# One hybrid decoder step: the first norm by sums of squares per token, and the dt products between the first chunk's two units

## The chip, the cores and the metric

The kernel runs on one core of a Trainium2 chip. The metric is the device time of one execution in microseconds (us), lower is better.

## The reference

The kernel computes two layers over 320 tokens (256 of a prompt, 64 of samples) of width 1024, in float32. Cut to what matters here:

```python
def rmsnorm(x, g):
    y = xf * lax.rsqrt(jnp.mean(xf * xf, axis=-1, keepdims=True) + EPS)
    return (y * g.astype(jnp.float32)).astype(x.dtype)

def parallel_mixer(hn, ...):
    proj = jnp.einsum('bld,de->ble', hn, w_in)          # 1024 x 3592
    q, f, i, og, z, xbc, dt = jnp.split(proj, SPLIT_IDX, axis=-1)   # dt: the last 8 columns
    ...
def trunk(...):
    for l in range(DEPTH):                              # 2 layers
        mix, ... = parallel_mixer(rmsnorm(h, norm_mix[l]), ...)
        h = h + mix
        hn = rmsnorm(h, norm_ffn[l])
        h = h + (swiglu(hn, ...) if l % 2 == 0 else moe_swiglu(hn, ...))
    return rmsnorm(h, norm_final), ...
```

## The kernel before

Activations lie transposed: `xT` has the 1024 features as 8 groups of 128 partitions and the 320 tokens as columns. Each engine has its own written-out list of instructions (`block.sync`, `gpsimd`, `scalar`, `vector`, and TensorE), and the lists meet only at counting semaphores `S(name)`. So the order of the lines of an engine is the order of its work, and a wait holds everything behind it on that engine.

**Weights** come in units of 1 MB through a ring of six buffers. SyncE's queue loads unit `u` (L435). ScalarE copies it to `spH`, rounded to the high part (`split_hi`, L591), VectorE subtracts to get the low part `spL` (`split_lo`, L944), and the next load into that buffer waits for `split_done`. `spH` and `spL` have two buffers each: `split_hi(u)` waits until TensorE has used unit `u-2`. A product is then three matmuls: high weights with `hnH` (L1505) and with `hnL` (L1506), low weights with `hnH` (L1584). A chunk of `w_in` is 512 output columns, two units of 512 input rows each; a layer has seven chunks (function `dense` on TensorE, 32 + 32 matmuls of high weights and 32 of low ones in a chunk). Of chunks 0 and 1 VectorE makes a convolution of four taps (L1046, L1049), which ScalarE then passes through Silu (L694, L695). Chunk 2 is the first without one.

**The start.** SyncE loads the three tiles of tokens `xin` (128, 128 and 64 tokens, L424), then units 0 and 1, then the table `stage` and the rest of `tab` (L428, L429), then units 2 and on. TensorE waits for all three tiles (`x_in` 48), transposes them in six groups of four into two PSUM banks in turn (L1549), and ScalarE copies each group to `xT` (L626). TensorE then turns two small arrays of vectors (`vin`, L1555; norm weights among them), of which layer 1's come by GpSimd's queue and layer 0's by ScalarE's (L392).

**A norm before** (`norm_t` on ScalarE and VectorE, `norm_mm` on TensorE): ScalarE squares four groups of `xT` and VectorE four. Then both split two units of weights (`before_rstd`). TensorE sums the squares over the partitions with eight float32 matmuls of a matrix of ones (L1521). ScalarE makes `rstd` from it (L606, L607). VectorE multiplies `xT` by the norm weight and `rstd` (eight instructions, L955). ScalarE copies the two halves to `hnH` (L610), VectorE subtracts to get `hnL` (L962).

**The dt products** (`narrow`, L1499 to L1501): 24 matmuls of 8 weight columns (`wnH`, `wnL`) with `hnH` and `hnL`. They stand ahead of chunk 0 on TensorE, and they wait for `setup_dve` 2, that is `wnL` (L982). Ahead of them stand eight small transposes of the convolution's state `cst` (L1563). At the end of chunk 0 their result is turned (L1538).

ScalarE rounds the table `stage` to `tabR` (L645) right after the first norm and its small set-up copies, ahead of the loading of the Silu table. TensorE needs `tabR` after the seven chunks (L1620).

## Time and profile before

| what | before |
|---|---|
| median of 3 executions | 1950.88 us (1950.7 to 1952.35) |
| the profiled execution, its own time | 1948.23 us |
| its span in the profile | 1946.5 us, 1.73 us less than its time |
| share of TensorE, VectorE, ScalarE in the chain that ended last | 89%, 7%, 2% |
| TensorE busy with matmuls | 1838.4 us, 94% of the span |
| VectorE busy | 1338.6 us, 69% |
| ScalarE busy | 1046.1 us, 54% |
| GpSimd busy | 85.1 us, 4% |
| mean granted clock of TensorE | 0.953 of full |

The first layer's input projection ends near 140 us and the second layer starts near 572 us; from about 890 us the experts run. A busy TensorE is not TensorE at its peak: at the lower clock the same matmul takes about twice as long. Times in the rows are from the start of the span.

### The profile page before, as it was taken

The page shows a single profiled execution, that of the slowest core. Times are in us where ns is not written, and L with a number is a line of the kernel's source. Part 1 is how long each engine was busy: PE and PEld are TensorE (multiplying, and loading weights), DVE is VectorE, ACT ScalarE, POOL GpSimd, SP SyncE. Part 2 cuts the span into 40 slices and gives each one's busy share as a digit, 9 for nine tenths or more (in the row PEclk, how much of TensorE's full clock was granted, in tenths as well). Part 3 has the DMA queues.
Part 4 walks back from the last instruction along what each step waited for, and adds up shares of the span by engine and source line. Part 5 has one row for each costly group of instructions (what it writes and reads, how often), then busy time and mean ns, then how long its engine had stood idle before and what let it go on. Part 6 is the DMA issues. An engine that isn't in the chain of part 4 may idle for free.

```text
span 1946.5 us, 25826 instructions
## 1 busy us (share of the span) xinstructions
PE 1838.4 (94%) x9949; PEld 1601.0 (82%) x9949; DVE 1338.6 (69%) x1160; ACT 1046.1 (54%) x924; POOL 85.1 (4%) x93
## 2 busy tenths in 40 slices
PE   6998988999889998987999999999999999999996
PEld 5997867999889988876888888888888888888885
DVE  3635554444355345536988889889888898888987
ACT  3443323333333442234677767776677767776775
POOL 2002120000000011211000000000000000000000
PEclk9998878999999978787999999999999999999998
DMA  7432134443462412135999999999999999999994
GB/s 241 140 123 55 35 95 132 146 147 115 120 190 87 152 41 54 45 103 201 338 364 326 355 340 344 367 331 353 364 330 353 328 354 368 327 351 334 353 357 146
DMA packets 267900, 452.62 MB, mean 233 GB/s; under 512 B 41258, under 2 KB 102946, under 8 KB 267832
## 3 DMA queue, kind: packets, MB, share of 16 engines
q1 hardware_dynamic: 266192, 448.83, 66.5%
q0 software_dynamic: 1376, 2.67, 0.7%
q8 instruction: 48, 0.79, 0.2%
q10 hardware_dynamic: 264, 0.17, 0.1%
q14 instruction: 20, 0.16, 0.0%
HBM read 440.66 MB, written 10.97 MB: 232 GB/s over the span
## 4 chain that ended last, share of the span: by engine, by line
PE 89%; DVE 7%; ACT 2%; issue 1%; DMA 1%; POOL 0%; SPq 0%; DVEq 0%; ACTq 0%
PE ps L1510 16%; PE ps L1511 16%; PE ps L2038 11%; PE ps L1505 8%; PE ps L1506 7%; PE ps L2053 5%; PE ps L1584 3%; PE ps L1969 3%; PE ps L1693 3%; PE ps L1678 2%; DVE cvt L1049 1%; PE ps L1984 1%; PE ps L2081 1%; DVE spL L944 1%; PE ps L1848 1%
## 5 line engine op out<-in xcount | busy, mean ns | idle before, releaser
L1401 DVE TENSOR_TENSOR spL<-ring,spH 128x2048 fp32r<-128x2048 f32 x339 | 771.5, 2292 | 113.0 <-ACT spH L873 112.9
L873 ACT ACTIVATE spH<-ring 128x2048 fp32r<-128x2048 f32 x339 | 648.6, 1916 | 124.9 <-PE ps L2053 64.8
L1510 PE MATMUL ps<-spH,XH 128*128 128x512 f32 x896 | 356.8, 398 | 1.5 <-DVE XL L1407 1.5
L1511 PE MATMUL ps<-spH,XL 128*128 128x512 f32 x896 | 352.0, 393 | 0.0
L944 DVE TENSOR_TENSOR spL<-ring,spH 128x2048 fp32r<-128x2048 f32 (+1 forms) x74 | 158.4, 2147 | 238.0 <-ACT spH L591 237.9
L1505 PE MATMUL ps<-hnH,spH 128*128 128x320 f32 x928 | 276.8, 313 | 13.7 <-DVE hnL L962 7.1
L1506 PE MATMUL ps<-hnL,spH 128*128 128x320 f32 x928 | 275.3, 311 | 0.0
L591 ACT ACTIVATE spH<-ring 128x2048 fp32r<-128x2048 f32 (+1 forms) x74 | 132.6, 1798 | 246.5 <-PE ps L1584 107.8
L2038 PE MATMUL ps<-spL,XH 128*128 128x512 f32 x896 | 241.8, 392 | 0.0
L1510 PEld LDWEIGHTS ps<-spH,XH 128*128 128x128 f32 x896 | 168.9, 188 | 37.8 <-issue 1.7
L2038 PEld LDWEIGHTS ps<-spL,XH 128*128 128x128 f32 x896 | 168.4, 188 | 36.8
L1511 PEld LDWEIGHTS ps<-spH,XL 128*128 128x128 f32 x896 | 169.0, 189 | 35.8
L1505 PEld LDWEIGHTS ps<-hnH,spH 128*128 128x128 f32 x928 | 176.3, 190 | 15.6 <-issue 15.4
L1510 PE MATMUL ps<-spH,hTH 128*128 128x512 f32 x448 | 178.8, 399 | 0.0
L1511 PE MATMUL ps<-spH,hTL 128*128 128x512 f32 x448 | 176.6, 394 | 0.0
L1506 PEld LDWEIGHTS ps<-hnL,spH 128*128 128x128 f32 x928 | 176.2, 190 | 0.3 <-issue 0.2
L2053 PE MATMUL ps<-spL,hTH 128*128 128x512 f32 x448 | 121.4, 393 | 0.0
L1510 PEld LDWEIGHTS ps<-spH,hTH 128*128 128x128 f32 x448 | 84.2, 188 | 19.4
L2053 PEld LDWEIGHTS ps<-spL,hTH 128*128 128x128 f32 x448 | 84.2, 188 | 19.3
L1511 PEld LDWEIGHTS ps<-spH,hTL 128*128 128x128 f32 x448 | 84.2, 188 | 18.7
L1584 PE MATMUL ps<-hnH,spL 128*128 128x320 f32 x576 | 90.3, 309 | 0.0
L1584 PEld LDWEIGHTS ps<-hnH,spL 128*128 128x128 f32 x576 | 86.0, 188 | 0.0
(323 smaller groups left out, 2094.0 us busy)
## 6 DMA issues: line engine op xcount, KB each, us to landing
ring<-in_w_exp_in_dram SPq DMA_DIRECT2D x227, 1024.0 KB, 6.7
ring<-in_w_exp_out_dram SPq DMA_DIRECT2D x112, 1024.0 KB, 6.4
ring<-in_w_in_dram SPq DMA_DIRECT2D x28, 1024.0 KB, 5.7
ring<-in_w_ffn_in_dram SPq DMA_DIRECT2D x22, 1024.0 KB, 5.2
ring<-in_w_ffn_out_dram SPq DMA_DIRECT2D x16, 704.0 KB, 4.4
ring<-in_w_out_dram SPq DMA_DIRECT2D x8, 1024.0 KB, 5.0
out_dram<-ring SPq DMA_DIRECT2D x32, 256.0 KB, 2.6
ring<-in_state_hgrn_dram SPq DMA_DIRECT2D x16, 256.0 KB, 3.7
```

Source lines behind the costliest of these rows:

```text
L591: A(spH[:, u % 2, 0:n], raw(u, n), ACT.Copy).then_inc(S("hi_done"), 1)
L873: A(esplit(j)[0], src, ACT.Copy).then_inc(S("hi_done"), 1)
L944: V.tensor_tensor(spL[:, u % 2, 0:n], raw(u, n), spH[:, u % 2, 0:n].bitcast(F32), ALU.subtract).then_inc(S("split_done"), 1)
L1401: V.tensor_tensor(lo, eslot(j)[0], hi.bitcast(F32), ALU.subtract).then_inc(S("split_done"), 1)
L1505: mm(out, w, x[0], start=start, stop=False)
L1506: return mm(out, w, x[1], start=False, stop=False)
L1510: mm(out, x[0], w, start=start, stop=False)
L1511: return mm(out, x[1], w, start=False, stop=False)
L1584: m = mm(ps[:, 4 * (c % 2) + i, 0:TOK], wL[:, k, i * P:(i + 1) * P], hnH[:, kk], start=False, stop=kk == KT - 1)
L1693: m = mm(out, vtk_of(t)[0:n, h * P:(h + 1) * P], flat(SCb[h % 2])[0:n, v * n:(v + 1) * n], start=v == 0, stop=v == nl and t != 1)
L2038: m = mm(ps[:, 2 * (c % 2) + i // 2, :], XH[:, kk], wL[:, k], start=False, stop=kk == KT - 1)
L2053: m = mm(ps[:, 6 + q, :], tH[:, f], wL[:, k, 512 * q:512 * q + 512], start=False, stop=c == EC - 1 and f == 3)
```

## The change

The first norm is made another way. ScalarE squares each tile of `xin` as it lands, with the sum over the features of each token as accumulated output (`xr`), and makes the factor of each token from three columns. VectorE, which now copies the transposes to `xT` from six PSUM banks, multiplies the identity by the factors (`xdg`), and TensorE multiplies a matrix of ones by these diagonals: that gives the row of factors in all partitions of PSUM bank 4, and VectorE's eight products read it there. VectorE makes both parts of `hnL` each ahead of the split of a unit. TensorE starts the transposes of a tile when that tile is there.

In both layers TensorE starts chunk 0 as soon as `hnL` allows, and the eight transposes of `cst` and the dt products (`turn_small`) stand between its two units. The small set-up of VectorE (`lbt`, `lbom`, `dtb`) moves behind the norm. SyncE loads `stage` and the rest of `tab` behind unit 3, not unit 1. ScalarE rounds `tabR` ahead of the splits of chunk 2 (`C_Q`).

```diff
@@ -44,6 +44,7 @@
 LV = 7
 LS = 3
 RING = 6
+X_BANKS = (2, 3, 5, 6, 7, 0)
 UN = 2048
 
 
@@ -263,6 +264,9 @@
         sq = put("sq", [P, KT, TOK], offset=arena)
         xin = put("xin", [P, 3, D], offset=arena + 4 * KT * TOK)
         vin = put("vin", [68, DEPTH, P], offset=arena + 4 * (KT * TOK + 3 * D))
+        xsq = put("xsq", [P, 3, D], offset=arena + 4 * 6 * D)
+        xdg = put("xdg", [P, 3, P], offset=arena + 4 * 9 * D)
+        xr = put("xr", [P, 2, 3], offset=arena + 4 * 9 * D + 2048)
         sqh = put("sqh", [P, H, TOK], offset=arena)
         sqs = put("sqs", [P, 4, TOK], offset=arena + 4 * H * TOK)
         rsh = put("rsh", [P, H, TOK], offset=arena + 8 * H * TOK)
@@ -421,10 +425,10 @@
 
             for t, (o, n) in enumerate(TILES):
                 src = a["x_prompt"][0, o:o + n] if t < 2 else a["x_sample"].rearrange("b s d -> (b s) d")
-                sp.dma_start(xin[0:n, t], src).then_inc(S("x_in"), 16)
+                sp.dma_start(xin[0:n, t], src).then_inc(S(f"x_in{t}"), 16)
             small = nr + 2 * P
             for u in range(PLAN["moe", 1]):
-                if u == 2:
+                if u == 4:
                     sp.dma_start(stage[:], a["table"][:, 0:nr]).then_inc(S("stage_in"), 16)
                     sp.dma_start(tab[:, 2 * P:], a["table"][:, small:]).then_inc(S("tab_in"), 16)
                 src, n, k = unit_src(u)
@@ -484,6 +488,7 @@
 
         @block.gpsimd
         def _(pool):
+            nc.gpsimd.memset(xr[:, 0], 1.0)
             nc.gpsimd.memset(eps[:], EPS).then_inc(S("eps_set"), 1)
             vectors(pool, 1)
             for l in range(DEPTH):
@@ -601,8 +606,6 @@
 
                     act.wait_ge(S("mixer_stored"), 1)
                 act.wait_ge(S("ss_mm"), k + 1)
-                if k == 0:
-                    act.wait_ge(S("eps_set"), 1)
                 own(A(rstd[:], ps[:, 0, 0:TOK], ACT.Ln, bias=eps[:, 0:1], scale=1.0 / D))
                 A(rstd[:], rstd[:], ACT.Exp, scale=-0.5).then_inc(S("rstd_done"), 1)
                 for half in range(2):
@@ -619,18 +622,23 @@
             tables(LN_EXP)
             vectors(act, 0)
 
+            act.wait_ge(S("eps_set"), 1)
             for t, (o, n) in enumerate(TILES):
-                for half in range(2):
-                    i = 2 * t + half
-                    act.wait_ge(S("xin_tr"), i + 1)
-                    A(xT[:, 4 * half:4 * half + 4, o:o + n],
-                      ps[:, 2 + i % 2, 0:4 * n].rearrange("p (k n) -> p k n", k=4), ACT.Copy
-                      ).then_inc(S("xT_done"), 1)
+                act.wait_ge(S(f"x_in{t}"), 16)
+                A(xsq[0:n, t], xin[0:n, t], ACT.Square, accum_out=xr[0:n, 0, t:t + 1]).then_inc(S("sq_done"), 1)
+            act.wait_ge(S("sq_done"), 3)
+            own(A(xr[:, 1], xr[:, 0], ACT.Ln, bias=eps[:, 0:1], scale=1.0 / D))
+            A(xr[:, 1], xr[:, 1], ACT.Exp, scale=-0.5).then_inc(S("rstd_done"), 1)
 
             for l in range(DEPTH):
                 u = PLAN["in", l]
                 if l == 0:
-                    norm_t(0, S("xT_done"), 5, sq, (u, u + 1))
+                    split_hi(u)
+                    for half in range(2):
+                        act.wait_ge(S("hn_f"), half + 1)
+                        A(hnH[:, 4 * half:4 * half + 4], sq[:, 4 * half:4 * half + 4], ACT.Copy
+                          ).then_inc(S("hnH_done"), 1)
+                    split_hi(u + 1)
 
                     act.wait_ge(S("small_in"), 16 * (4 * DEPTH + 1))
                     A(bc[:, :, 1], bc[:, :, 1], ACT.Exp).then_inc(S("setup_act"), 1)
@@ -639,11 +647,6 @@
                     A(lbt[:, 0:2], lbt[:, 0:2], ACT.Exp).then_inc(S("setup_act"), 1)
                 else:
                     norm_t(2, S("down_evac"), 4, sq, (u, u + 1))
-                if l == 0:
-
-                    act.wait_ge(S("stage_in"), 16)
-                    A(tabR[:], stage[:], ACT.Copy).then_inc(S("tab_round"), 1)
-
                 tables(SILU)
                 act.wait_ge(S("cst_tr"), l + 1)
                 for k in range(8):
@@ -652,6 +655,10 @@
                       ).then_inc(S("pads_done"), 1)
 
                 for c in range(7):
+                    if l == 0 and c == C_Q:
+
+                        act.wait_ge(S("stage_in"), 16)
+                        A(tabR[:], stage[:], ACT.Copy).then_inc(S("setup_act"), 1)
                     if c < C_I:
                         split_hi(u + 2 * c + 2)
                         split_hi(u + 2 * c + 3)
@@ -963,20 +970,44 @@
                                     hnH[:, 4 * half:4 * half + 4].bitcast(F32), ALU.subtract
                                     ).then_inc(S("hnL_done"), 1)
 
+            for t, (o, n) in enumerate(TILES):
+                for half in range(2):
+                    i = 2 * t + half
+                    dve.wait_ge(S("xin_tr"), i + 1)
+                    V.tensor_copy(xT[:, 4 * half:4 * half + 4, o:o + n],
+                                  ps[:, X_BANKS[i], 0:4 * n].rearrange("p (k n) -> p k n", k=4)).then_inc(S("xT_done"), 1)
+            dve.wait_ge(S("rstd_done"), 1)
+            dve.wait_ge(S("id_in"), 16)
+            for t, (o, n) in enumerate(TILES):
+                ins = V.tensor_scalar(xdg[0:n, t, 0:n], ident[0:n, 0:n], xr[0:n, 1, t:t + 1], None, ALU.mult)
+            ins.then_inc(S("xdg_done"), 1)
+
             dve.wait_ge(S("vec_tr"), 1)
             own(V.tensor_copy(vec[:], ps[:, 1, 0:DEPTH * 68].rearrange("p (l n) -> p l n", l=DEPTH)))
-
-            own(V.tensor_tensor(lbt[:, 2], vec[:, 0, 64:68], vec[:, 1, 64:68], ALU.max))
-            own(V.tensor_tensor(lbt[:, 0], vec[:, 0, 64:68], lbt[:, 2], ALU.subtract))
-            V.tensor_tensor(lbt[:, 1], vec[:, 1, 64:68], lbt[:, 2], ALU.subtract).then_inc(S("setup_dve"), 1)
-            own(V.memset(lbom[:, 0, 0], 0.0))
-            own(V.memset(lbom[:, 0, 1], 1.0))
-            own(V.memset(dtb[:], 0.0))
 
             for l in range(DEPTH):
                 u = PLAN["in", l]
                 if l == 0:
-                    norm_t(0, 0, 0, sq, S("xT_done"), 6, (u, u + 1))
+                    dve.wait_ge(S("xT_done"), 6)
+                    dve.wait_ge(S("ss_mm"), 1)
+                    for i in range(KT):
+                        ins = V.scalar_tensor_tensor(out=sq[:, i], in0=xT[:, i], scalar=vec[:, 0, i:i + 1],
+                                                     in1=ps[:, 4, 0:TOK], op0=ALU.mult, op1=ALU.mult)
+                        if i % 4 == 3:
+                            ins.then_inc(S("hn_f"), 1)
+                    for half in range(2):
+                        dve.wait_ge(S("hnH_done"), half + 1)
+                        V.tensor_tensor(hnL[:, 4 * half:4 * half + 4], sq[:, 4 * half:4 * half + 4],
+                                        hnH[:, 4 * half:4 * half + 4].bitcast(F32), ALU.subtract
+                                        ).then_inc(S("hnL_done"), 1)
+                        split_lo(u + half)
+
+                    own(V.tensor_tensor(lbt[:, 2], vec[:, 0, 64:68], vec[:, 1, 64:68], ALU.max))
+                    own(V.tensor_tensor(lbt[:, 0], vec[:, 0, 64:68], lbt[:, 2], ALU.subtract))
+                    V.tensor_tensor(lbt[:, 1], vec[:, 1, 64:68], lbt[:, 2], ALU.subtract).then_inc(S("setup_dve"), 1)
+                    own(V.memset(lbom[:, 0, 0], 0.0))
+                    own(V.memset(lbom[:, 0, 1], 1.0))
+                    own(V.memset(dtb[:], 0.0))
 
                     dve.wait_ge(S("setup_act"), 2)
                     V.tensor_tensor(wnL[:, 0:DEPTH], wnr[:, 0:DEPTH], wnH[:, 0:DEPTH].bitcast(F32), ALU.subtract
@@ -1517,7 +1548,7 @@
             def norm_mm(k, sqv):
                 for i in range(KT):
                     if i % 4 == 0:
-                        pe.wait_ge(S("sq_done") if i == 0 else S("sq2_done"), k + 1)
+                        pe.wait_ge(S("sq_done") if i == 0 else S("sq2_done"), k + 3 if i == 0 else k)
                     m = mm(ps[:, 0, 0:TOK], onesf, sqv[:, i], start=i == 0, stop=i == KT - 1)
                 m.then_inc(S("ss_mm"), 1)
 
@@ -1539,14 +1570,11 @@
                 return m
 
             pe.wait_ge(S("id_in"), 16)
-            pe.wait_ge(S("x_in"), 48)
             for t, (o, n) in enumerate(TILES):
+                pe.wait_ge(S(f"x_in{t}"), 16)
                 for half in range(2):
-                    i = 2 * t + half
-                    if i >= 2:
-                        pe.wait_ge(S("xT_done"), i - 1)
                     for k in range(4):
-                        m = nc.tensor.transpose(ps[:, 2 + i % 2, k * n:(k + 1) * n],
+                        m = nc.tensor.transpose(ps[:, X_BANKS[2 * t + half], k * n:(k + 1) * n],
                                                 xin[0:n, t, (4 * half + k) * P:(4 * half + k + 1) * P],
                                                 ident[0:n, 0:n])
                     m.then_inc(S("xin_tr"), 1)
@@ -1555,14 +1583,22 @@
                 m = nc.tensor.transpose(ps[:, 1, 68 * l:68 * l + 68], vin[:, l], ident[0:68, 0:68])
             m.then_inc(S("vec_tr"), 1)
 
+            pe.wait_ge(S("xdg_done"), 1)
+            for t, (o, n) in enumerate(TILES):
+                m = mm(ps[:, 4, o:o + n], onesf[0:n], xdg[0:n, t, 0:n], start=True, stop=True)
+            m.then_inc(S("ss_mm"), 1)
+
             for l in range(DEPTH):
-                norm_mm(2 * l, sq)
-
-                pe.wait_ge(S("cst_in"), 16 * (l + 1))
-                for k in range(8):
-                    m = nc.tensor.transpose(ps[:, 6, 24 * k:24 * k + 24], cst[:, k * P:(k + 1) * P], ident[0:24, 0:24])
-                m.then_inc(S("cst_tr"), 1)
-                narrow(l, ps[:, 7], 4 * l)
+                if l:
+                    norm_mm(2 * l, sq)
+
+                def turn_small():
+
+                    pe.wait_ge(S("cst_in"), 16 * (l + 1))
+                    for k in range(8):
+                        m = nc.tensor.transpose(ps[:, 6, 24 * k:24 * k + 24], cst[:, k * P:(k + 1) * P], ident[0:24, 0:24])
+                    m.then_inc(S("cst_tr"), 1)
+                    narrow(l, ps[:, 7], 4 * l)
 
                 def dense(u, c, inputs=None, mid=None):
 
@@ -1590,7 +1626,7 @@
                     return m
 
                 for c in range(7):
-                    if c == 0:
+                    if c == 0 and l:
                         pe.wait_ge(S("rstd_done"), 2 * l + 1)
                     if c == 1:
 
@@ -1598,7 +1634,8 @@
                         pe.wait_ge(S("dt_evac"), l + 1)
                     if c >= 2:
                         pe.wait_ge(S("proj_evac"), 6 * l + c - 1)
-                    dense(PLAN["in", l] + 2 * c, c).then_inc(S("used"), 1)
+                    dense(PLAN["in", l] + 2 * c, c, (S("hnL_done"), 4 * l) if c == 0 else None,
+                          turn_small if c == 0 else None).then_inc(S("used"), 1)
                     if c == 0:
                         narrow_turn(l, dtT, ps[:, 7]).then_inc(S("dt_mm"), 1)
 
@@ -1617,7 +1654,7 @@
                     (o, n), i = TILES[t], LT(l, t)
                     if t == ORDER[0]:
                         pe.wait_ge(S("lf_done"), H * (l + 1))
-                        pe.wait_ge(S("tab_round"), 1)
+                        pe.wait_ge(S("setup_act"), 4)
                     else:
 
                         pe.wait_ge(S("v_done"), i)
```

## Rows read from the trace of the kernel before

**Rows 1.** The chain that ended last, 0 to 120 us: start, us, what.

```profile
2.94 17.25 DMA ring<-in_w_in_dram
20.21 1.92 ACT spH L591
22.15 2.29 DVE spL L944
24.44 3.70 DVE sq L955 x8
28.14 2.83 DVE hnL L962 x2
...
31.23 0.43 PE ps L1499
31.66 0.27 PE ps L1500
...
35.95 0.15 PE ps L1501
...
48.26 2.36 PE ps L1584 x16
50.70 1.92 ACT spH L591
...
80.81 1.81 ACT spH L591
```

**Rows 2.** The timeline, 0 to 75 us: start, us, engine, line, what, idle before.

```profile
0.75 0.91 SPq L424 DMA_DIRECT2D xin<-in_x_prompt_dram  x2
...
2.32 1.28 SPq L435 DMA_DIRECT2D ring<-in_w_in_dram  x2
...
4.50 0.52 POOL L392 DMA_DIRECT2D vin<-in_lb_param_dram  x1
...
8.40 5.11 PE L1549 MATMUL ps<-tab,xin 128*128 128x128 f32 x24 [8.40 <-DMA xin<-in_x_sample_dram]
...
13.96 0.30 DVE L967 COPY vec<-ps 128x136 f32<-128x136 f32 x1 [13.96 <-PE ps L1555]
...
15.13 7.57 PE L1521 MATMUL ps<-sq,tab 128*128 128x320 f32 x16 [1.21 <-ACT sq L597]
...
26.32 1.27 ACT L610 ACTIVATE hnH<-sq 128x1280 fp32r<-128x1280 f32 x1 [2.56 <-DVE sq L955]
...
29.75 1.47 ACT L645 ACTIVATE tabR<-stage 128x1536 fp32r<-128x1536 f32 x1
```

**Rows 3.** Tile xin: from issue to landing of its three loads.

```profile
DMA to landing us min/median/max: 4.3/5.6/6.6
```

**Rows 4.** Tile ring, load of unit 0 (2.3 to 2.9 us): issue to landing.

```profile
DMA to landing us min/median/max: 9.7/9.7/9.7
```

**Rows 5.** DMA issues, 0 to 10 us: KB each, us to landing.

```profile
vin<-in_lb_param_dram POOLq DMA_DIRECT2D x1, 2.0 KB, 5.9
```

**Rows 6.** ScalarE's timeline near the end, last tile of the final norm.

```profile
1939.99 1.06 ACT L924 ACTIVATE junk<-ht 64x1024 f32<-64x1024 f32 x1 [0.51 <-DVE ht L1415]
...
1941.49 0.20 ACT L927 ACTIVATE fss<-fss 64x1 f32<-64x1 f32 x1
```

**Rows 7.** Line L1161, a VectorE product with one operand in PSUM.

```profile
L1161 DVE SCALAR_TENSOR_TENSOR cvT<-cvT,dcol,ps x24: 275/342/348, 244.2 to 826.3; 128x128 f32<-128x128 f32 x16, 128x64 f32<-128x64 f32 x8
```

**Rows 8.** TensorE by stretches: busy, granted clock, DMA share, GB/s.

```profile
34.00:35.00 1.00, 1.00 (x6) 0.57 1.05 387
...
587.00:588.00 1.00, 1.00 (x6) 0.59 0.00 0
```

**Rows 9.** TensorE's timeline at the start of layer 1.

```profile
576.09 0.67 PE L1563 MATMUL ps<-tab,cst 24*128 24x24 f32 x8
583.34 0.42 PE L1499 MATMUL ps<-hnH,wnH 128*8 128x320 f32 x1 [6.58 <-DVE hnL L962]
```

**Rows 10.** Waits of TensorE, 50 to 90 us: total, times, longest.

```profile
PE ps L1505 <- ACT spH L591: 2.8, 2, 1.4
```

## The prediction

> **What bounds the kernel now.** I read the page first: the chain that ended last is TensorE's for nearly nine tenths, so what the change can give must come out of a stretch where that chain runs through something else. The chain in order of time finds it [rows 1]. Until 20.2 us it waits for a load (unit 1), then it goes ScalarE's split, VectorE's split, the eight products of the norm, `hnL`, and TensorE starts its first real products, those of dt, at 31.23 us. From there to the end of chunk 0 at 50.62 us (48.26 + 2.36) it is TensorE alone. Then come ScalarE's split of unit 3 and VectorE's convolutions, up to the split of unit 6 at 80.81 us, and TensorE again for seven chunks less two. So two things count: when the first products start, and what is put into the stretch from 50.7 to 82.6 us, where TensorE has idle time only because ScalarE and VectorE are late [rows 10].
>
> Note what the chain says of the load: unit 1 lands at 20.2 us, and the norm stands behind its two splits on VectorE. The norm itself needs only `xin`, which is there at 8.4 us [rows 2]. The other load of that time, unit 0, lands at 2.32 + 9.7 = 12.0 us [rows 2, 4].
>
> **The start, step by step.** Tile 0 lands at 0.75 + 4.3 = 5.05 us [rows 2, 3], tile 2 at 8.4 us. TensorE's 24 transposes took 5.11 us with their waits for ScalarE, 0.21 us each, so from 8.4 us the last eight end by 10.1 us, the others lie before. VectorE's copies: 0.30 us for 136 columns out of PSUM [rows 2]. The lines that move data at one column in 1.04 ns leave a fixed part of 0.16 us; so 0.69 us for 512 columns, 0.42 for 256, and the last is done at about 10.5 us. The copies move from ScalarE to VectorE and neither is short of time there.
>
> ScalarE: from the start of the square of a tile to the end of the factor's Exp the final norm takes 1941.49 + 0.20 - 1939.99 = 1.70 us [rows 6], so the factors are there at 10.1 us. The two earlier squares, 1.25 us each, fit in 5.05 to 8.4 us. The factor waits for VectorE's copies: three products of at most 128 columns, 0.2 us each as an estimate from the 0.30 us copy, so `xdg` is done at 11.1 us. Ahead of the diagonals on TensorE stand the transposes of the vectors, and the last of these lands at 4.50 + 5.9 = 10.4 us [rows 2, 5]; they end at 10.8 us, hidden. ScalarE's vectors were issued before. The diagonals are 320 columns in all; eight sums of 320 took 7.57 us [rows 2], so 0.95 us, and the factor row is in PSUM at 12.2 us with the hand-over.
>
> The eight products take 3.70 us [rows 1], to 15.9 us. Their operand now lies in PSUM. Products with one operand in PSUM took 342 ns for 128 columns [rows 7]; the 3.70 us for eight of 320 is 463 ns each, with overlap, and the difference fits the 192 columns; I add nothing, with 0.5 us as the upper bound. `hnH` of the first half: 1.27 us [rows 2] behind the split of unit 0, which ends at 12.0 + 1.9 = 13.9 us, ahead of the fourth product at 14.05 us; so it is done at 15.4 us, before VectorE is free. `hnL` of the first half takes 2.83 / 2 = 1.4 us [rows 1], to 17.35 us, and TensorE starts at **17.5 us instead of 31.23: 13.7 us earlier**.
>
> Here the Trainium skill speaks against the change (VectorE: DVE Perf Modes, on the trn2 errata): its table gives an instruction of VectorE a fixed part of 120 cycles with a PSUM source and 58 with an SBUF one. By it the eight products would take 8 x 0.065 = 0.5 us more, an estimate from the page. The rows above show no such part.
>
> **Between 17.5 us and the end of chunk 0.** TensorE's work is the same except for its order: 24 dt products and 96 of the chunk, 19.4 us from 31.23 to 50.62. The eight `cst` transposes, before in idle time, now lie on the path: 0.67 us [rows 9], I take 0.6 net of overlap. The 19.4 us has a slow stretch in it. The granted clock was half (1.2 GHz) until 34.86 us, 3.6 us after the start, and the spacing of these matmuls went from 0.27 to 0.15 us there [rows 1, 8]. In layer 1 the same start at 583.34 rose at 587.8, 4.5 us after [rows 8, 9]. Each us at the lower clock costs 0.45 us (1 - 0.147 / 0.267). I take 4.5 us, 0.4 us more than before. The bounds: no slow stretch at all gains 0.45 x 4.5 = 2.0 us, if nothing else waits; 7.6 us of it, as long as the sums at 15.13 us ran, most of them slow [rows 2], costs 1.4 us.
>
> The Trainium skill (TensorE: Matmul & The Clock Gate, Part 1) says that an idle array falls to half rate and that the moment of the rise is not tied to the kernel's start but varies from run to run. The two rises above agree with it as far as two go; it changes only the spread.
>
> Do the products wait for anything new? Second half of chunk 0: TensorE gets to it after 48 matmuls (9.1 us with 4.5 slow, 26.6 us), the transposes (27.2) and dt (30.7). Unit 1, landed at 20.2, is split by 22.1 and 24.4 us. Cover 6 us. dt: `wnL` is behind VectorE's split at 24.4, six short set-up instructions (0.2 us each at most) and itself 0.3, so 25.8 us. Cover 1.4 us; it goes if the clock is up early, and then the chunk ends at 25.8 + 3.5 + 7.05 = 36.4 us. That is the cap of the gain. ScalarE loads the Silu table and pads `xbc` in the meantime; its split of unit 2 comes at 28 us and TensorE needs it at 38. The loads: units 2 and 3 go ahead of `stage` and land earlier, later units do not move; before, the chain names no load after unit 1's [rows 1], and units 4 and on are wanted only once chunk 1 has begun. Behind ScalarE's wait for unit 1 stand only the set-up copies.
>
> So chunk 0 ends at 17.5 + 19.4 + 0.6 + 0.4 = **37.9 us instead of 50.6: 12.7 us earlier**. All that follows hangs on that point by the same waits (the split of unit 3, `dt_evac`, the convolutions), so it is carried on.
>
> **What is given back.** Rounding `tabR` takes 1.47 us [rows 2]. Before it stood where TensorE waited for nothing of ScalarE. Now it stands between the last Silu of chunk 1 and the split of unit 6, at the point that is 80.81 us in the chain [rows 1], and TensorE is already idle there, half of 2.8 us [rows 10]. Nothing covers it, and after it TensorE is the bound with no slack to take it back: **1.4 us lost**. Layer 1: the products start at the same `hnL` (the first 12 dt products had only needed the first half too), and are the same in number; the `cst` transposes were in an idle time of 6.58 us [rows 9] and are now on the path: **0.6 us lost**. ScalarE's pads and VectorE's `dtT` copy there now stand ahead of the splits of unit 2, which have half a chunk of cover, 48 matmuls or 7 us.
>
> Sum: -12.7 + 1.4 + 0.6 = -10.7 us. Against the profiled execution's own time, 1948.23, that is 1937.5. The median of the runs shown lies 2.65 us above that execution, so the forecast of the median is 1950.88 - 10.7 = **1940.2 us**.
>
> **The rivals.**
> - *The start is later than the sum.* The transposes of the vectors stand ahead of the diagonals on TensorE; they ran by 13.96 us [rows 2], and ScalarE's own seven loads show no landing time. If they were only just in, the diagonals start at 13.7 us, not 11.1. For it: nothing but the missing row; against: GpSimd's, issued later, land at 10.4. Gain 8.1 us, 1942.8. Chance 0.12.
> - *The clock is up early, or the rounding is hidden.* Then the cap above: 36.4 us, 1.5 us more, or 1.4 more; 1938.7. Chance 0.15.
> - *Slower.* The lower clock stays. A chunk that starts after idle time at half rate and is not raised costs 0.12 us for each of its matmuls: 120 of them would take 32 us from 17.5 us, the end at 50.1, and with the 2.0 us given back the time is 1952.4; each further chunk of 96 at that rate costs 11.5 us more. The point from which it is slower by over 0.2%, 1954.8, is 2.4 us on, some 5 us (2.4 / 0.45) of the lower clock in chunk 1. For it: both starts after idle time ran at the lower clock. Against: both rises came within 5 us of work [rows 8]. 1955 to 1964, the latter with all of chunk 1. Chance 0.02.
> - *The change does not start the products earlier*, because something that I don't see (a load, a bank) holds `hnL` until unit 1 is split: the start is then 24.4 + 2.8 = 27.2 us, gain 4.0 - 1.0 - 2.0 = 1 us, 1949.9, no change. Against: in the new order the first half of `hnL` stands ahead of the wait for unit 1 on both engines. Chance 0.04.
>
> **How the numbers follow.** The forecast has 0.67, the rivals the rest. A difference under 0.2% (3.9 us) can hardly be told from no change. Low end: the cap with the rounding hidden, 1940.2 - 1.5 - 1.4 = 1937.3, less one us for the runs' own spread (1.65 us), 1936.3. High end: late vectors, 1942.8, with the 0.5 us for PSUM and the 1.4 us for a longer slow stretch, 1944.7. Range 1936.3 to 1944.7. Faster holds the forecast and the first two rivals, 0.94; same 0.04; slower 0.02.
>
> **What the profile after would show.** L1505's first matmul near 17.5 us and the end of chunk 0 near 38 us; the diagonals near 11 us; no wait before dt at 27 us; L645 just ahead of the split of unit 6, with TensorE idle there for 2.9 us, not 1.45; `cst` between the units. Wrong would be: a start after 20 us (then the waits of VectorE's first products name the cause), or a gap from chunk 0's end to unit 6's split that is not the 30.1 us of before plus 1.4.

## The result, and the profile after

| what | after | before |
|---|---|---|
| median of 4 executions each | 1931.18 us (1922.91 to 1934.33) | 1950.79 us (1947.58 to 1952.35) |
| ratio, 95% interval | 0.9907 [0.9882, 0.9933] | 1 |
| the profiled execution, span | 1922.91 us, 1921.1 us | 1948.23 us, 1946.5 us |
| TensorE busy, mean granted clock | 1821.1 us, 0.961 | 1838.4 us, 0.953 |
| mean of all executions measured in this study | 1932.7 us (22, standard error 0.7) | 1948.6 us (81, standard error 0.3) |

The forecast was 1940.2 us, 10.7 us less than before. It came out faster, as forecast, but by more than the range allowed. The last line of the table is the one to explain: over all executions the change gives 15.9 us, with a standard error of 0.75. The first profiled execution of the new kernel is a lucky one (25 us less than that of the kernel before).

The chain of the kernel after, 0 to 85 us, to be read against [rows 1]:

```profile
5.54 3.69 PE ps L1577 x16
9.25 1.04 DVE xT L977 x2
...
10.64 0.64 DVE xdg L982 x3
11.32 1.85 PE ps L1588 x6
13.30 3.75 DVE sq L994 x8
17.06 1.41 DVE hnL L1000
...
36.18 2.36 PE ps L1620 x16
38.62 1.92 ACT spH L596
...
70.00 1.90 ACT spH L596
```

The load of unit 1 is gone from the chain, the loads of the start and the norm stand in its place, and chunk 0 ends at 36.18 + 2.36 = 38.54 us, 12.1 us earlier than the 50.62 of before. The split of unit 6 starts at 70.00 us instead of 80.81, 10.8 us earlier. TensorE's timeline of the kernel after shows the start, and ScalarE's the table on the path:

```profile
11.32 1.84 PE L1588 MATMUL ps<-xdg,tab 128*128 128x128 f32 x6 [0.35 <-DVE xdg L982]
...
18.52 0.63 PE L1536 MATMUL ps<-hnH,spH 128*128 128x320 f32 x1 [5.36 <-DVE hnL L1000]
```

```profile
68.47 0.24 ACT L702 ACTIVATE cvT<-cvt 128x64 f32<-128x64 f32 x1
68.62 1.47 ACT L661 ACTIVATE tabR<-stage 128x1536 fp32r<-128x1536 f32 x1
70.00 3.70 ACT L596 ACTIVATE spH<-ring 128x2048 fp32r<-128x2048 f32 x2
```

TensorE waits for those two splits for 2.8 us at the longest, against 1.4 before [rows 10] (waits of TensorE after, 30 to 85 us: total, times, longest):

```profile
PE ps L1536 <- ACT spH L596: 4.1, 2, 2.8
```

In this trace the sum holds within 0.6 us so far. The rest came from stretches that the prediction took as unchanged. The table below divides the span at the starts of the same seven VectorE instructions in each trace (143.0, 290.4, 571.7, 612.4, 851.3, 941.6, 1926.8 us in the kernel before, the last of them the last but one of the splits of the experts' weights). "The end" goes from there to the start of VectorE's last instruction. Each number is a difference of two starts, in us:

```
stretch (before's us)  0-143  143-290  290-572  572-612  612-851  851-942  942-1927  the end
before                 143.0   147.4    281.3     40.7    238.9     90.3    985.2     15.0
before, again (2)      143.7   145.6    282.4     41.4    234.4     90.9    985.1     15.0
before, again (3)      143.1   150.9    280.9     41.2    236.6     91.5    985.2     15.0
after                  133.8   139.2    281.0     42.0    232.2     90.1    985.2     12.9
after, again           133.3   148.4    281.4     42.0    232.2     90.1    985.1     12.9
after, again (2)       132.4   149.4    281.3     41.5    232.9     90.9    985.2     12.9
after, again (3)       133.1   151.9    281.3     42.0    232.2     90.1    985.2     12.9
```

Four columns differ by kernel: the start (-10.1 on the mean), layer 1's first chunk (+0.8), the rest of layer 1's mixer (232.4 against 236.6, -4.2), and the end (-2.1). They sum to -15.6; the other columns differ by under 1 us on their means. That holds for the stretch from 143 to 290 us only because of one trace. It differs by execution: 139.2 in the first trace of the new kernel, 145.6 to 151.9 in all six others of the table, and the three repeats of the new kernel have 149.9 on the mean where the kernel before has 148.0. That is the luck of the profiled execution, and a reason to take means of three or four traces with care. The windows of TensorE's row show what the differences are made of (us, busy, granted clock, DMA share, GB/s). Before, 143 us on and layer 1's mixer:

```profile
143.00:290.40 147.40, 131.82 (x846) 0.83 0.24 58
...
612.40:851.30 238.90, 219.83 (x1394) 0.86 0.27 76
```

After, the same two:

```profile
133.80:273.00 139.20, 125.49 (x845) 0.87 0.26 64
...
596.10:828.30 232.20, 212.72 (x1395) 0.89 0.28 78
```

The same matmuls, a different granted clock. The lower level is half of the full clock, so a mean of 0.86 over 238.9 us is 2 x 0.14 x 238.9 = 67 us at 1.2 GHz, 0.89 over 232.2 us is 51 us; 16 us x 0.45 is 7 us, and 6.7 were measured.

### The profile page after: what moved, and what is told of

Its sections match the earlier page's. It is cut to its first block, busy times and chain, and to the rows that moved or that the text cites. A ratio compares the mean times of both kernels' runs of the same rounds, so it can differ in the third digit from the quotient of the medians.

```text
span 1921.1 us, 25818 instructions
## 1 busy us (share of the span) xinstructions
PE 1821.1 (95%) x9939; PEld 1588.3 (83%) x9939; DVE 1339.3 (70%) x1168; ACT 1044.5 (54%) x923; POOL 85.7 (4%) x94
## 4 chain that ended last, share of the span: by engine, by line
PE 89%; DVE 6%; ACT 2%; issue 2%; DMA 0%; POOL 0%; DVEq 0%; ACTq 0%
PE ps L1541 16%; PE ps L1542 16%; PE ps L2075 11%; PE ps L1536 8%; PE ps L1537 8%; PE ps L2090 5%; PE ps L1620 3%; PE ps L2006 3%; PE ps L1730 2%; DVE cvt L1080 1%; PE ps L1715 1%; PE ps L2021 1%; PE ps L2118 1%; PE ps L1885 1%; PE ps L1768 1%
## 5 line engine op out<-in xcount | busy, mean ns | idle before, releaser
L596 ACT ACTIVATE spH<-ring 128x2048 fp32r<-128x2048 f32 (+1 forms) x74 | 132.8, 1799 | 232.4 <-PE ps L1620 93.9
```

The costliest lines, as they stand in the source:

```text
L596: A(spH[:, u % 2, 0:n], raw(u, n), ACT.Copy).then_inc(S("hi_done"), 1)
```

## The experiments

My theory after the result: the start and the table are near the forecast (-10.1), and the rest comes by the clock. The first traces made it narrower: 2.1 us come from the place of VectorE's instructions in its list, 4.2 from the clock in layer 1's mixer, and the remainder is luck. Rivals: the extra is luck altogether; one part of the change alone gives it; the table's rounding or layer 1's new order costs another sum than forecast; it hangs on how the whole program is aligned to the clock's rises.

**The changed kernel again**, three times, each beside runs of the kernel before on the same chip, and the kernel before with a profile, twice (before, again in the table).

> The changed kernel once more, with more executions. Theory of the clock: the local gain is near 10 us and the rest of each execution's distance to the kernel before is 0.45 times its difference in time at the lower clock; so executions scatter by several us, their time follows their mean granted clock, and the mean gain over many is anything from 10 to 20 us. Rival, a fixed second gain: every execution is 19 to 21 us faster than the kernel before, whatever its clock says.

> The changed kernel a third time, as the measure for the other three on the same chip. By what the traces showed so far: 12 to 17 us faster than the kernel before in the mean (10.7 of the start, 2.0 of VectorE's wait at the end, less 0.7 in layer 1, the rest by the clock).

> The changed kernel once more, as the measure for the next two on the same chip: 14 to 17 us faster than before in the mean.

> The kernel before, for a second trace of it. If its trace of the first part is chance in layer 1's mixer (every other trace but one is 2 to 7 us shorter between 612 and 851 us), this one is shorter there too by 2 to 6 us; if the new order is what shortens that stretch, it takes the same 238.9 us again.

> A third trace of the kernel before, with the same expectation as before2.

Measured: 1932.51, 1932.15 and 1935.03 us, ratios 0.9923 [0.991, 0.9936], 0.9918 [0.99, 0.9937], 0.9929 [0.9909, 0.995]; the kernel before profiled at 1945.02 and 1951.01. By the means on each chip the three gains are 14.5, 16.2 and 14.0 us. Their stretches are in the table above. The 25 us of the first profile were luck by about 10; a gain of 14 to 16 us is not. Layer 1's mixer took 234.4 and 236.6 us in the two new traces of the kernel before: so the 238.9 us of its first trace were in part chance, as the first branch of that expectation has it, though both are still above the 232.2 to 232.9 of the new kernel.

**The norm alone, and the order alone.**

```diff
 norm_only: the kernel after, in both layers
+                turn_small()
                 for c in range(7):
-                    dense(PLAN["in", l] + 2 * c, c, (S("hnL_done"), 4 * l) if c == 0 else None,
-                          turn_small if c == 0 else None).then_inc(S("used"), 1)
+                    dense(PLAN["in", l] + 2 * c, c).then_inc(S("used"), 1)
 order_only: the kernel before, its cst and narrow lines made turn_small
-                    dense(PLAN["in", l] + 2 * c, c).then_inc(S("used"), 1)
+                    dense(PLAN["in", l] + 2 * c, c, (S("hnL_done"), 4 * l) if c == 0 else None,
+                          turn_small if c == 0 else None).then_inc(S("used"), 1)
```

> The new norm alone: cst transposes and dt products stand ahead of chunk 0 again in both layers. By the waits, the first dt product then starts when wnL is there, near 25.5 us, 5.7 us earlier than before (31.2); chunk 0 ends 5.7 us earlier, less 1.4 us for tabR: 4.3 us gained up to unit 6. Layer 1 is as before. Rival, the new order brings nothing of its own: then it is as fast as the changed kernel, 10.7 us gained at unit 6. Second rival, the missing 9 us come from the new order in layer 1: then this kernel has none of them.

> The kernel before with the dt products and cst transposes between the two units of chunk 0, nothing else. By the waits, chunk 0 starts at the first half of hnL, near 29.7 rather than 31.2 us for the dt products, 1.5 us earlier, and pays 0.6 us in each layer for the cst transposes: a total of -0.3 us, no difference. Rival: the order brings the missing 9 us somewhere later, by the clock after the norm of layer 1 or else.

norm_only keeps the later load of the table and its rounding ahead of chunk 2. Measured: 1943.37 us, 0.9973 [0.996, 0.9987], and 1943.38 us, 0.9982 [0.997, 0.9993]. Together they give 15.9 us, singly 5.0 and 3.5 (means). The start shows why (waits and TensorE's timeline of norm_only):

```profile
PE ps L1599 <- DMA cst<-in_state_conv_dram: 9.2, 1, 9.2
...
PE ps L1530 <- DVE wnL L1013: 3.0, 1, 3.0
```

```profile
25.49 0.44 PE L1530 MATMUL ps<-hnH,wnH 128*8 128x320 f32 x1 [3.03 <-DVE wnL L1013]
```

With the old order `wnL`, which stands behind the split of unit 1 on VectorE, holds the first product until 25.49 us; with the old norm `hnL` comes late whatever the order. The order alone moved the end of the start by 0.1 us only; its 3.5 us are in its trace a shorter mixer in layer 1 (232.9 us, against a mean of 236.6).

**The table rounded early**, behind unit 2's split, and a repeat on another chip.

```diff
-                    if l == 0 and c == C_Q:
-                        act.wait_ge(S("stage_in"), 16)
-                        A(tabR[:], stage[:], ACT.Copy).then_inc(S("setup_act"), 1)
                     if c < C_I:
                         split_hi(u + 2 * c + 2)
+                        if l == 0 and c == 0:
+                            act.wait_ge(S("stage_in"), 16)
+                            A(tabR[:], stage[:], ACT.Copy).then_inc(S("setup_act"), 1)
```

> As the changed kernel, but tabR is rounded in chunk 0, between ScalarE's splits of units 2 and 3, where ScalarE waits for TensorE anyway. By my sum it gets back 1.4 us: the split of unit 6 starts 9.2 us rather than 10.7 after the last Silu minus... that is, TensorE's idle time ahead of unit 6 goes from 2.9 to 1.45 us. Rival, the rounding is absorbed later: that wait gets shorter and the end of layer 0's input projection does not move. In the total it may drown in the clock's scatter.

> The kernel with tabR rounded in chunk 0 again, for a mean over twice as many executions: by the waits 1.4 us faster than the changed kernel beside it.

Measured: 1932.21 us, 0.9928 [0.9907, 0.995], and 1931.16 us, 0.9922 [0.99, 0.9944]. The rounding moves to 30.32 us, the wait goes back to that of before, and the first 143 us take 130.9 and 130.8 us against 132.4 to 133.8 (ScalarE's timeline and TensorE's waits of the first of the two):

```profile
30.32 1.55 ACT L662 ACTIVATE tabR<-stage 128x1536 fp32r<-128x1536 f32 x1
```

```profile
PE ps L1535 <- ACT spH L596: 2.8, 2, 1.4
```

The 1.4 us are real where they arise. In the totals they can't be seen: the mean of 12 executions is 1933.1 us, that of the changed kernel's 22 is 1932.7; the standard error of the difference is about 1.4 us.

**Layer 1's order put back**: the small products ahead of its first chunk (l1_old), or only the `cst` transposes (cst_idle). A third kernel joins the first to the early table (best).

```diff
 l1_old: the kernel after
+                if l:
+                    turn_small()
...
-                          turn_small if c == 0 else None).then_inc(S("used"), 1)
+                          turn_small if c == 0 and not l else None).then_inc(S("used"), 1)
 best: the same and the edit of tab_early
 cst_idle: in layer 1 the eight transposes of cst ahead of chunk 0, narrow between its units
```

> The changed kernel with layer 1's cst transposes and dt products ahead of chunk 0 again, as in the kernel before; layer 0 stays changed. Theory of the clock: the new order in layer 1 costs 0.6 to 0.8 us by itself, but it moves the mixer of layer 1 against the clock's falls, and that is where the changed kernel's traces lose 10 us less at the lower clock (700 to 750 us of before), 4.6 us; so this kernel loses that part, and is slower than the changed one by 4.6 - 0.8 = 3 to 4 us. Rival, the waits alone count: it is faster than the changed kernel by 0.6 to 0.8 us.

> The changed kernel with layer 1's eight cst transposes back in TensorE's idle time ahead of chunk 0, its dt products still between the units. By the waits alone 0.6 us faster than the changed kernel. By the clock, the mixer comes 0.6 us earlier behind the rise than in the changed kernel, and the 4.6 us of layer 1's mixer may be lost: up to 4 us slower.

> The changed kernel with tabR rounded in chunk 0 and layer 1 in the old order: both of the things that were given back are taken off. By the waits 1.4 + 0.7 = 2.1 us faster than the changed kernel on the same chip, 14 to 19 us faster than before. Rival: the clock's scatter hides it, or the new order in layer 1 is worth more by the clock than the 0.7 us.

Measured: 1931.97 us, 0.9911 [0.9897, 0.9926]; 1932.65 us, 0.9916 [0.9898, 0.9935]; 1933.60 us, 0.9923 [0.9906, 0.994]. Layer 1's first chunk takes 41.3 us again in all three, so the 0.6 us is there as forecast. But the mixer behind it took 234.3, 234.3 and 237.2 us. First chunk and mixer together are then 275.6 us in l1_old and cst_idle, 1.3 us more than the mean of the changed kernel's four traces. The totals can't show so small a loss: the means, 1933.3 and 1933.2 us, are 0.6 and 0.5 us above the changed kernel's, with standard errors of 1.7 and 2.0. My expectation that l1_old would lose 3 to 4 us was not borne out. best, expected 2.1 us faster than the changed kernel on its chip (again2), has a mean of 1934.3 us against 1932.4 (standard error of the difference 1.7), so those 2.1 us are not seen.

**Eight and 24 idle transposes added**, where the changed kernel has its eight: in the kernel before at layer 1 (pad8, pad24), in the changed kernel at layer 0 (shift8, shift24). Their result is used by nothing.

```diff
 in dense, between the two units
+                            if u == PLAN["in", 1]:      # shift8, shift24: PLAN["in", 0]
+                                for k in range(8):      # or 24
+                                    nc.tensor.transpose(ps[:, 5, 24 * (k % 8):24 * (k % 8) + 24],
+                                                        cst[:, (k % 8) * P:(k % 8 + 1) * P], ident[0:24, 0:24])
```

> The kernel before with eight more cst transposes (into an unused bank) between the two units of chunk 0 of layer 1: 0.6 us of added work on TensorE's path and nothing taken away. Theory of the clock: the mixer of layer 1 comes 0.6 us later behind the clock's rise, as with the new order, and less of it is at the lower clock: faster than before by 1 to 4 us, though it does more. Rival, the waits alone count: 0.6 us slower.

> The same with 24 more transposes, 1.8 us of added work at most. Theory of the clock: not proportional to the work; anything between 3 us faster and 5 us slower, and what is not 1.5 to 1.8 us is in the time at the lower clock behind 690 us. Rival, the waits alone count: 1.5 to 1.8 us slower, with the low-clock time of the kernel before.

> The changed kernel with eight more cst transposes in chunk 0 of layer 0: 0.5 us of added work, everything behind it 0.5 us later. If the 4 to 5 us beyond the waits belong to the change as such, this kernel is 0.5 us slower than the changed one. If they come from how the mixers lie against the clock's falls, they are another number here, anywhere from 0 to 8.

> The same with 24 more, 1.5 us of added work. As such: 1.5 us slower than the changed kernel. By the clock: another number, from 5 us slower to 3 us faster.

Measured: 1948.36 us, 0.9991 [0.9982, 1.0001]; 1949.60 us, 1.0003 [0.9988, 1.0019]; 1934.90 us, 0.9937 [0.9918, 0.9957]; 1935.57 us, 0.9936 [0.9917, 0.9955]. pad8 adds work to the kernel before, and its mixer takes less time; l1_old takes work out of the changed kernel's path, and its mixer takes more (windows of TensorE; first pad8):

```profile
614.00:846.90 232.90, 213.89 (x1397) 0.88 0.27 78
```

```profile
607.40:841.70 234.30, 214.82 (x1397) 0.88 0.27 77
```

The times of this stretch over all twenty traces:

```
layer 1's first chunk      mixer behind it, us
without the eight in it    238.9 234.4 236.6 (before)  239.2 norm_only  234.3 dve_pad  234.3 l1_old
                           234.3 cst_idle  237.2 best
with the eight in it       232.2 232.2 232.9 232.2 (after)  232.2 232.0 tab_early  232.9 order_only
                           232.9 pad8  232.9 shift8  235.6 shift24  235.3 warm
with 24                    235.3 pad24
```

None of the first eight is under 234.3, nine of the other eleven are under 233. So what stands between the start of layer 1 and its mixer does change the mixer's clock. But shift24 and warm have that same code and 235.6 and 235.3 us. First chunk and mixer together, the eight traces without them have 277.3 us on the mean and the eleven with them 274.9: 2.4 us, with a standard error of 0.8.

A second thing that differs between executions of one kernel moves the mixer as much: the moment of the clock's rise in layer 1's first chunk. It comes either about 16.2 us after that stretch begins (the granted clock of the stretch is then 0.92) or 17.0 to 17.5 us after (0.88). Without the eight transposes in the chunk, the mixer took 238.9 and 239.2 us behind the early rise (before, norm_only) and 234.3 to 237.2 behind the late one; with them it took 232.9 behind the early rise all four times (again2, order_only, pad8, shift8), and 232.0 to 232.2, 235.3 or 235.6 behind the late one. So one trace of a kernel isn't a measure of its mixer.

In the totals, pad8 got 1.4 us (means, standard error 0.8), not the 3 that its trace shows, and pad24 is 0.4 us slower (standard error 1.5) for 1.5 us of work in its first chunk. shift8 and shift24 (+0.9 and +1.8 us on the means against again3 on the same chip, for 0.5 and 1.5 us of work) give no sign that the gain hangs on how layer 0 is aligned.

**Eight small instructions on VectorE**, in the kernel before, behind its set-up: nothing but the length of the list changes.

```diff
                     own(V.tensor_tensor(lbom[:, 1, 0], lbt[:, 1], lbt[:, 3], ALU.mult))
                     V.tensor_tensor(lbom[:, 1, 1], lbt[:, 0], lbt[:, 3], ALU.mult).then_inc(S("setup_dve"), 1)
+                    for _ in range(8):
+                        own(V.memset(cvt[:, 0, 0:4], 0.0))
```

> The kernel before with eight tiny memsets more on VectorE in its idle time of layer 0, and nothing else. In the kernels with the old list of VectorE it stands idle for 1.9 us behind the experts' loop, released by nothing that the profile shows, and in those with the new norm, whose list is eight instructions longer, it does not. Theory: this wait hangs on where the instructions lie, and goes: 2.0 us faster than before. Rival: the wait has another cause in the norm or is chance, and stays: no change.

Measured: 1945.88 us, 0.9988 [0.9974, 1.0002], means 1945.9 against 1948.6 (standard error of the difference 1.1). VectorE at the end, before, after and dve_pad:

```profile
1930.50 2.29 DVE L1401 TENSOR_TENSOR spL<-ring,spH 128x2048 fp32r<-128x2048 f32 x1 [0.16 <-ACT spH L873]
1934.72 3.38 DVE L1415 SCALAR_TENSOR_TENSOR ht<-ps,rk,ht 128x512 f32<-128x512 f32 x5 [1.93 <-issue]
```

```profile
1907.24 2.29 DVE L1432 TENSOR_TENSOR spL<-ring,spH 128x2048 fp32r<-128x2048 f32 x1 [0.16 <-ACT spH L880]
1909.45 3.37 DVE L1446 SCALAR_TENSOR_TENSOR ht<-ps,rk,ht 128x512 f32<-128x512 f32 x5
```

```profile
1929.22 2.29 DVE L1403 TENSOR_TENSOR spL<-ring,spH 128x2048 fp32r<-128x2048 f32 x1 [0.17 <-ACT spH L873]
1931.43 3.37 DVE L1417 SCALAR_TENSOR_TENSOR ht<-ps,rk,ht 128x512 f32<-128x512 f32 x5
```

Between the last split and the sums that follow, VectorE waits 1.93 us with the releaser "issue", so for nothing that the trace shows. Eight instructions more, which run at 31.6 us, 1900 us earlier, take the wait away, and the stretch falls from 15.0 to 12.9 us. All six traces with VectorE's old list (the kernel before three times, order_only and the two pads) have 15.0 us there; the fourteen with a longer list have 12.9.

**TensorE kept busy before the first product**: four sums over `xT`, whose result nobody reads, behind the diagonals.

```diff
+            pe.wait_ge(S("xT_done"), 6)
             pe.wait_ge(S("xdg_done"), 1)
...
+            for i in range(4):
+                mm(ps[:, 5, 0:TOK], onesf, xT[:, i], start=i == 0, stop=i == 3)
```

> The changed kernel with four float32 sums of 320 columns into an unused bank on TensorE behind the diagonals, in its idle time of 13.2 to 18.5 us. If the lower clock of the first products costs what my sum says (0.45 us for each us), chunk 0 ends up to 1.4 us earlier, near 37.1 to 38.0 us. Rival: the clock is as low as without it, or the dt products then wait for wnL; chunk 0 ends as before.

Measured: 1932.86 us, 0.9933 [0.9908, 0.9957]. TensorE's timeline:

```profile
11.37 1.81 PE L1589 MATMUL ps<-xdg,tab 128*128 128x128 f32 x6 [0.99 <-DVE xdg L982]
13.11 4.63 PE L1592 MATMUL ps<-xT,tab 128*128 128x320 f32 x8
18.54 0.41 PE L1536 MATMUL ps<-hnH,spH 128*128 128x320 f32 x1 [0.80 <-DVE hnL L1000]
18.79 0.30 PE L1537 MATMUL ps<-hnL,spH 128*128 128x320 f32 x1
```

The clock is up by the first product: the trace has its rise at 17.7 us, in the eleven other traces with the new norm and layer 0's new order the rise that ends the slow products comes at 21.5 to 24.0 us. Chunk 0 ends at 37.10 us, 1.4 us before the 38.54 of the changed kernel's first trace and 1.9 us before the mean of its four, and the first 143 us take 130.9. The total again doesn't show it (mean 1933.5 against again2's 1932.4). So no version with both parts of the change is told by its total from the changed kernel on the same chip.

## Why the prediction was wrong

**What bounds the kernel now** held: the stretch before the first product and the point at unit 6 were the two places that count, and norm_only and order_only show that the gain needs both parts.

**The start, step by step.** The mechanism was right. Tile 0 was there by 5.40 us (forecast 5.05), when ScalarE starts its square. TensorE's transposes began at 5.54: what they waited for last was the load of `tab`, which holds the identity, a wait that the prediction did not have.

```profile
5.40 1.06 ACT L628 ACTIVATE xsq<-xin 128x1024 f32<-128x1024 f32 x1 [2.92 <-DMA xin<-in_x_prompt_dram]
5.54 4.72 PE L1577 MATMUL ps<-tab,xin 128*128 128x128 f32 x24 [5.54 <-DMA tab<-in_table_dram]
```

The factors were there at 10.37 (10.1), `xdg` at 11.3 (11.1), and the vectors were in time, so the rival of the late vectors fell. The one term clearly mis-sized is the diagonals: 1.84 us, not 0.95. I had taken the rate of the eight sums [rows 2]. The clock explains little of the difference, for the sums too ran at the lower clock until 21.2 us; at that level the starts of their matmuls lie 0.53 us apart, so 320 columns cost 1.07 us. The rest is that six short matmuls in three pieces don't overlap as one long row does: they start 0.21 to 0.37 us apart, and the last takes another 0.42 us to its end. That is read from the records; no run tested it. In the trace of best, where the clock had risen to 2.4 GHz at 10.0 us, the same six took

```profile
11.28 1.07 PE L1587 MATMUL ps<-xdg,tab 128*128 128x128 f32 x6 [0.77 <-DVE xdg L981]
```

The eight products took 3.75 us with their operand in PSUM, 3.70 before [rows 1]; the 0.5 us more that I worked out from the Trainium skill (VectorE: DVE Perf Modes, the trn2 errata) is not in this case's traces. The argument from [rows 7] did not show that beforehand: 463 less 342 ns is 121 ns, where 192 columns at 1.04 ns are 200. The first product started at 18.52 us, 1.0 late. With the clock up for the diagonals it came at 17.71 us in best and at 17.73 in again2, a trace of the changed kernel itself.

**Between 17.5 us and the end of chunk 0.** 20.0 us against a forecast of 20.4. The lower clock lasted from 18.52 to 21.7 us, 3.2 us, not 4.5; the `cst` transposes took 0.67 us at 27.20, and dt followed at 27.81 with no wait for `wnL`, whose cover of 1.4 us was 2.3. Chunk 0 ended 12.1 us earlier, not 12.7 (39.5 us, 11.1 earlier, in the second execution). The short slow stretch was luck: in the changed kernel's three repeats it lasted 5.2 to 5.5 us, 4.9 us on the mean of the four, near the 4.5 of the forecast. On the means (four traces against three) the first product came 12.9 us earlier, not 13.7, and the end of chunk 0 11.9, not 12.7. The Trainium skill says that the rise is run-variable (TensorE: Matmul & The Clock Gate, Part 1), and the traces agree: 21.7, 24.0, 23.0 and 23.7 us in the changed kernel's four.

**What is given back.** Right. -10.8 us at unit 6 against -11.3 (-10.5 on the means), tab_early moves just that 1.4 us, and layer 1's first chunk is 0.8 us longer against 0.6. One thing more: the longer idle time ahead of unit 6 (2.8 us) was followed in four of the traces that have it (after, cst_idle, shift8, shift24) by a fall of the clock, here with a spacing of 0.27 us from 73.19 to 76.39 (chain after), at a cost of 1.5 us; in again, again2 and again3 it wasn't, nor in l1_old.

```profile
73.00 0.20 PE ps L1537
73.19 0.27 PE ps L1536
...
76.39 0.19 PE ps L1536
76.58 0.15 PE ps L1537
```

**The step that failed** is "All that follows hangs on that point by the same waits ..., so it is carried on", with "after it TensorE is the bound with no slack". It took every microsecond after unit 6's split, but for the 0.6 in layer 1, as unchanged, and put the difference there at nothing. The runs showed otherwise in two places.

- *The end: 2.1 us, shown.* The prediction read the end of the chain as TensorE's and did not look at VectorE's 1.93 us "issue" in the last 16 us. dve_pad takes it away alone.
- *Layer 1's mixer: 4.2 us in the traces; its cause stays open in part.* The instructions are the same, the granted clock is 0.89 or 0.88 where before had 0.86 to 0.88. That eight transposes of 0.6 us can shorten it is what the traces of pad8, order_only, l1_old and cst_idle agree in; that the moment of the rise in the chunk ahead does as much is in them too. That these transposes are the cause of 4 us in the totals is not shown. l1_old and cst_idle, whose mixers of 234.3 us are 2.3 shorter than the mean of before, should gain 10.1 + 2.1 + 2.3 = 14.5 us by this account (less 0.2 for the first chunk), and their means gain 16.0 and 16.1, no less than the changed kernel. norm_only should gain 4.7 + 2.1, less the 2.6 us by which its mixer is longer, so 4.2, and gains 5.0; pad8 should gain 3 us and gains 1.4; dve_pad should gain 2.1 for the end and 2.3 for its mixer and gains 2.6; order_only's 3.5 are as its trace says. One trace of each and standard errors of 0.8 to 1.9 us in the gains are too coarse to settle it.

So of the 15.9 us the start, layer 1's first chunk and the end explain 11.4. Of the 4.5 left, the traces place 4.2 in layer 1's mixer, and there the granted clock differs and nothing else that was found. How much of it belongs to the change and how much to where the clock's rises happened to fall, there and from 143 to 290 us, stays open.

The rivals: the late vectors and a load or bank that holds `hnL` are refuted by the start at 18.52 us. The lower clock ended 3.2 to 5.5 us after the first product, so the slower case did not come near. The rival of an early clock did not happen in the changed kernel. warm makes it happen, and there it is worth 1.4 us to the end of chunk 0 against the first trace, which is 0.45 times the 3.2 us that this trace had of the lower clock. That the cap said 1.5 is a coincidence: it rested on dt waiting for `wnL`, and in warm `wnL` was ready at 25.93 us and dt started behind the `cst` transposes at 26.45 with no wait.

The level of the forecast was off too: it stood on the median of three executions, 1950.88 us, while the mean of 81 is 1948.6. Compared as differences, 10.7 us were forecast and 15.9 came. The terms that the prediction summed gave 9.3 us (10.1 less 0.8), 1.4 less than it said; the end gave 2.1, and the 4.5 of the stretches far behind the change came on top.

## What to carry to other kernels

A sum over the chain can be right where it was made: here it held within 0.8 us for the first 70 us. What it leaves out is that in a kernel whose TensorE falls to 1.2 GHz in its idle times, several us can hang on when the clock rises. Take the range's width from the stretches with a low mean clock, however far they lie from the change, and judge an edit of 1 to 2 us by the starts of the same instructions in several traces of each kernel, not by the total. Before a change alters the length of an engine's list, look for idle time with the releaser "issue" on that engine: it can go or come with the place of the instructions alone.

## What the runs showed of the hardware

- A stretch of the same instructions took 139.2 to 153.0 us (143 to 290 us, twenty traces), and its length follows the granted clock, 0.87 in the shortest; the third repeat of the changed kernel has 151.9 us at 0.78:

```profile
133.10:285.00 151.90, 139.11 (x845) 0.78 0.24 59
```

  The Trainium skill (TensorE: Matmul & The Clock Gate, Part 1) puts the penalty of a rise at under 1% of a kernel's span. One such stretch alone varies here by 13.8 us, 0.7% of this span. That figure is for one rise, and a stretch here holds several.
- The lengths of the mixer's stretch come in steps: 232.2, 232.9, 234.3, 235.3 recur to 0.1 us in different kernels. The moment of the clock's rise ahead of it goes with them: every 232.9 has the early one, every 232.2 and 234.3 the late one.
- VectorE stood still for 1.93 us between two instructions, released by nothing that the trace shows, just behind the long list of the experts, and the shift of eight instructions removed it. Which boundary of its code it was isn't known from these runs.
- The 24 float32 transposes at the start are enough to raise the clock in some executions and not in others. In again2, tab_early, tab_early2, norm_only, shift8, shift24 and best it rose at 8.3 to 10.0 us, when TensorE had done nothing but transposes since 5.0 to 5.5 us, and fell at 11.7 to 13.4 us, near the end of the diagonals. In after, again, again3, l1_old and cst_idle it was still low at the first product, at 18.3 to 18.5 us. In warm, with four float32 sums more (4.63 us) behind the diagonals, it was up at 17.7 us.
